# Hybrid decoder step on one core: order of bias, gather and first products in the experts' sums

## What is computed

```python
def expert_block(args):
    xb, e = args
    gu = xb @ w_gate_up[e] + b_gate_up[e]
    gt, up = gu[..., :D_EXPERT], gu[..., D_EXPERT:]
    gt = jnp.minimum(gt, SWIGLU_LIMIT)
    up = jnp.clip(up, -SWIGLU_LIMIT, SWIGLU_LIMIT)
    act = (up + 1) * (gt * jax.nn.sigmoid(gt * SWIGLU_ALPHA))
    return act @ w_down[e] + b_down[e]
...
out = jnp.zeros((N + 1, D), jnp.float32).at[slot_tok].add(ys.astype(jnp.float32) * slot_gate[:, None])[:N]
```

## Time and profile before

| | |
|---|---|
| median of 3 runs | 1282.88 us (1281.44 to 1283.17) |
| span of the profiled execution | 1278.8 us; an own time of that execution is not given |
| PE busy | 1208.2 us (94%) |
| DVE, ACT, POOL busy | 341.3, 208.4, 87.1 us |
| all transfers | 458.76 MB, mean 359 GB/s |
| chain that ended last | PE 62%, DMA 29%, DVE 5%, ACT 2% |

### The profile page before, as it was taken

The page is one execution under the profiler, slowest core; times in us unless marked ns, Lnnn a source line. Parts: engine busy times, 40 slices in busy tenths (PEclk is TensorE's granted clock), DMA queues, the critical chain, the costliest instruction groups (busy, mean ns, idle before and its releaser), DMA issues.

```text
span 1278.8 us, 18587 instructions
## 1 busy us (share of the span) xinstructions
PE 1208.2 (94%) x7592; PEld 594.0 (46%) x7592; DVE 341.3 (27%) x655; ACT 208.4 (16%) x421; POOL 87.1 (7%) x64
## 2 busy tenths in 40 slices
PE   6999999989999999999998989899898989898997
PEld 5877789875543433434333333324242433333332
DVE  1068497466411111111111111011111111111102
ACT  3133253320310111011011001000110101010002
POOL 0162003711000000000000000000000000000001
PEclk9999999999999999999999999999999999999999
DMA  9878460148699999999999999999999999999994
GB/s 316 197 249 283 144 222 12 37 177 322 279 379 427 428 428 425 429 427 428 426 428 427 427 426 429 428 426 427 429 428 426 427 428 427 428 427 428 428 426 190
DMA packets 52656, 458.76 MB, mean 359 GB/s; under 512 B 7092, under 2 KB 10844, under 8 KB 28004
## 3 DMA queue, kind: packets, MB, share of 16 engines
q1 hardware_dynamic: 49972, 452.22, 86.1%
q0 software_dynamic: 1824, 5.12, 1.7%
q10 hardware_dynamic: 784, 0.28, 0.1%
HBM read 453.74 MB, written 3.82 MB: 358 GB/s over the span
## 4 chain that ended last, share of the span: by engine, by line
PE 62%; DMA 29%; DVE 5%; ACT 2%; POOL 1%; issue 1%; SPq 0%; DVEq 0%; ACTq 0%; POOLq 0%
DMA ring<-in_w_gate_up 29%; PE ps L1901 24%; PE ps L1414 9%; PE ps L1922 7%; PE ps L1834 6%; PE ps L1881 3%; PE ps L1739 2%; PE ps L1843 2%; PE ps L1910 1%; DVE work L916 1%; PE ps L1390 1%; PE ps L1726 1%; DVE ring L916 1%; DVE work L954 1%; PE ps L1667 1%
## 5 line engine op out<-in xcount | busy, mean ns | idle before, releaser
L1901 PE MATMUL ps<-ring,work 128*64 128x512 f32 x1456 | 328.2, 598 | 32.0 <-DMA ring<-in_w_gate_up 30.0
L1901 PEld LDWEIGHTS ps<-ring,work 128*64 128x64 f32 x1456 | 101.3, 137 | 237.4 <-issue 192.6
L1304 DVE TENSOR_SCALAR work<-ps 128x512 f32<-128x512 f32 x32 | 22.1, 692 | 528.6 <-PE ps L1901 528.6
L1414 PE MATMUL ps<-work,ring 128*128 128x264 f32 x672 | 156.4, 392 | 2.2 <-ACT work L551 2.2
L1901 PE MATMUL ps<-work 128*64 128x512 f32 x592 | 132.7, 594 | 10.5 <-DMA work<-in_w_gate_up 10.5
L1414 PEld LDWEIGHTS ps<-work,ring 128*128 128x128 f32 x672 | 127.7, 192 | 28.2 <-issue 6.7
L1922 PE MATMUL ps<-ring,work 128*64 128x512 f32 x608 | 137.5, 597 | 0.2
L1922 PE MATMUL ps<-work 128*64 128x512 f32 x416 | 93.3, 594 | 0.2 <-DMA work<-in_w_down 0.2
L1322 DVE SCALAR_TENSOR_TENSOR work<-work 128x512 f32<-128x512 f32 x32 | 24.0, 751 | 241.0 <-ACT work L787 241.0
L1901 PEld LDWEIGHTS ps<-work 128*64 128x64 f32 x592 | 42.3, 137 | 94.0 <-issue 87.6
L1922 PEld LDWEIGHTS ps<-ring,work 128*64 128x64 f32 x608 | 41.3, 137 | 93.2 <-issue 89.6
(11 more groups left out here) (276 smaller groups left out, 900.1 us busy)
## 6 DMA issues: line engine op xcount, KB each, us to landing
ring<-in_w_gate_up SPq DMA_DIRECT2D x91, 2048.0 KB, 36.5
ring<-in_w_down SPq DMA_DIRECT2D x38, 2048.0 KB, 40.1
work<-in_w_gate_up SPq DMA_DIRECT2D x37, 2048.0 KB, 36.8
work<-in_w_down SPq DMA_DIRECT2D x26, 2048.0 KB, 39.5
ring<-in_w_in SPq DMA_DIRECT2D x5, 3072.0 KB, 16.6
ring<-in_w_out SPq DMA_DIRECT2D x1, 4096.0 KB, 13.0
ring<-in_w_in SPq DMA_DIRECT2D x2, 1536.0 KB, 8.7
ring<-in_cache_k SPq DMA_DIRECT2D x16, 192.0 KB, 7.5
```

Of the source, the lines that this page charges most:

```text
L1304: v.tensor_scalar(gt, PS[BG][:, :], LIMIT, None, ALU.min).then_inc(S_("gt"), 1)
L1414: last_ = mm(psum(job, T), w, hT[:, k, :], start=k == 0, stop=k == KD - 1)
L1901: last = mm(PS[bnk][g * 64:g * 64 + 64, :], lhs, UNIT[n % 9][:, w0 + base + g * 512:w0 + base + (g + 1) * 512], start=False, stop=k == KD - 1)
```

## The change

Three things are moved. (1) The gate and up sums now open with their first product (start=True at k = 0), and `bias` adds to them after k = 1, in both experts; `first_bias` and the bias calls between the stages are gone. (2) The second half of a pair's gather is no longer done in the pair before, but in the pair's own first `gate_up`, right behind the bias; ACT's copy of it moves to the head of the pair. (3) Ahead of the first pair, the sample rows' b_down term goes to bank BY in place of BU, and DVE makes the gates before it adds that term.

```diff
--- before.py
+++ after.py
@@ -748,18 +748,17 @@
                 nc.scalar.activation(gsT[g * 64:g * 64 + NE], PS[BX][0:NE, 0:NB], ACT.Copy).then_inc(S_("gate_s_out"), 1)
             route_exp(2)
 
-            def gathered(P, half, count, b=BX):
+            def gathered(P, half, count):
 
                 act.wait_ge(S_("xg_full"), count)
                 nc.scalar.activation(XG[P % 2][:, half, :, :, OWN:SLOT],
-                                     PS[b][:, :].rearrange("p (c e s) -> p c e s", c=4, e=2)[:, :, :, OWN:SLOT], ACT.Copy)\
+                                     PS[BX][:, :].rearrange("p (c e s) -> p c e s", c=4, e=2)[:, :, :, OWN:SLOT], ACT.Copy)\
                   .then_inc(S_("xgT_out"), 1)
 
             for h_ in range(2):
                 for e_ in range(2):
                     A_(nc.scalar.activation(XG[0][:, h_, :, e_, 0:OWN], h2T[:, 4 * h_:4 * h_ + 4, S:T], ACT.Copy))
-            for h_ in range(2):
-                gathered(0, h_, h_ + 1, (BX, BY)[h_])
+            gathered(0, 0, 1)
             for h_ in range(2):
                 A_(nc.scalar.activation(XG[1][:, h_, :, :, 0:OWN], XG[0][:, h_, :, :, 0:OWN], ACT.Copy))
 
@@ -790,13 +789,13 @@
                 with act.Fori(0, NE // 4) as four:
                     for q in range(2):
                         pr = act.snap(p * (NE // 2) + four * 2 + q)
+                        gathered(q, 1, pr * 2 + 2)
                         sigmoid(pr * 2)
                         gathered(q + 1, 0, pr * 2 + 3)
                         act_transposed(pr * 2)
                         act.wait_ge(S_("selgT_full"), pr + 1)
                         nc.scalar.activation(selgT_e[0], PS[BY][:, 0:256], ACT.Copy)
                         nc.scalar.activation(selgT_e[1], PS[BY][:, 256:512], ACT.Copy).then_inc(S_("selgT_out"), 1)
-                        gathered(q + 1, 1, pr * 2 + 4)
                         sigmoid(pr * 2 + 1)
                         expert_rows(pr * 2, pr * 12 + 19)
                         act_transposed(pr * 2 + 1)
@@ -1286,12 +1285,12 @@
             V(v.tensor_scalar(thr, marks, mcount, None, ALU.is_lt))
             V(v.tensor_reduce(mcount, thr, AX.X, ALU.add))
             V.ready(v.tensor_copy(npass[:, :], mcount), "npass", 1)
+            gates(1)
+            gates(2)
             dve.wait_ge(S_("samp_bias"), 1)
             dve.wait_ge(S_("samp_x"), 2)
-            V(tt(accs[0:NB], PS[BU][0:NB, :], accs[0:NB], ALU.add))
-            V.ready(tt(accs[64:64 + NB], PS[BU][64:64 + NB, :], accs[64:64 + NB], ALU.add), "samp_out", 1)
-            gates(1)
-            gates(2)
+            V(tt(accs[0:NB], PS[BY][0:NB, :], accs[0:NB], ALU.add))
+            V.ready(tt(accs[64:64 + NB], PS[BY][64:64 + NB, :], accs[64:64 + NB], ALU.add), "samp_out", 1)
 
             for b in range(1, PASSES):
                 V(v.tensor_scalar(posx[:, :, b * NE:(b + 1) * NE], posx[:, :, 0:NE], float(-FREE * b), None, ALU.add))
@@ -1827,11 +1826,11 @@
             pe.wait_ge(S_("sel_r"), 3)
             mm(rk[:, 1, :], C["before"], selr[:, 1, :], start=False, stop=False)
             done(mm(rk[:, 2, :], C["ones"], selr[:, 1, :], start=False, stop=True), "rk")
-            def gather(half, b=BX):
+            def gather(half):
 
                 for c in range(4):
                     for m in range(2):
-                        last = mm(PS[b][:, c * 128:(c + 1) * 128], h2[:, m, half * 512 + (c // 2) * 256 + c % 2:half * 512 + (c // 2 + 1) * 256:2],
+                        last = mm(PS[BX][:, c * 128:(c + 1) * 128], h2[:, m, half * 512 + (c // 2) * 256 + c % 2:half * 512 + (c // 2 + 1) * 256:2],
                                   sel[:, m].rearrange("p e s -> p (e s)"), start=m == 0, stop=m == 1)
                 last.then_inc(S_("xg_full"), 1)
 
@@ -1840,31 +1839,20 @@
                 pe.wait_ge(S_("pick"), count)
                 for i, g in ((0, 0), (1, 1), (0, 1), (1, 0)):
                     q = slice(i * NE, (i + 1) * NE)
-                    mm(PS[(BG, BU)[i]][g * 64:g * 64 + 64, :], pick[q, :], ebias[q, g * 512:(g + 1) * 512], start=True, stop=False)
-
-            def first_bias(i):
-
-                bank_free((BG, BU)[i])
-                q = slice(i * NE, (i + 1) * NE)
-                for g in range(2):
-                    mm(PS[(BG, BU)[i]][g * 64:g * 64 + 64, :], pick[q, :], ebias[q, g * 512:(g + 1) * 512], start=True, stop=False)
+                    mm(PS[(BG, BU)[i]][g * 64:g * 64 + 64, :], pick[q, :], ebias[q, g * 512:(g + 1) * 512], start=False, stop=False)
 
             pe.wait_ge(S_("gate_s_out"), 2)
             pe.wait_ge(S_("ld_bdown"), 32)
-            bank_free(BU)
+            bank_free(BY)
             for g in range(2):
                 q = slice(g * 64, g * 64 + NE)
-                last = mm(PS[BU][g * 64:g * 64 + NB, :], gsT[q], yS[q, :], start=True, stop=True)
+                last = mm(PS[BY][g * 64:g * 64 + NB, :], gsT[q], yS[q, :], start=True, stop=True)
             last.then_inc(S_("samp_bias"), 1)
-            pe.wait_ge(S_("pick"), 1)
-            pe.wait_ge(S_("ld_ebias"), 32)
-            first_bias(0)
             pe.wait_ge(S_("sel"), 1)
             gather(0)
-            bank_free(BY)
-            gather(1, BY)
-            pe.wait_ge(S_("samp_out"), 1)
-            first_bias(1)
+            pe.wait_ge(S_("ld_ebias"), 32)
+            bank_free(BG)
+            bank_free(BU)
             pe.wait_ge(S_("xgT_out"), 1)
             pe.wait_ge(S_("gate"), 3)
             for m in range(2):
@@ -1887,9 +1875,12 @@
             def gate_up(i, e_, pr, landed):
 
                 for k in range(KD):
-                    if e_ and k == 4:
-                        pe.wait_ge(S_("actT_out"), pr * 2 + 2)
-                        gather(1)
+                    if k == 2:
+                        bias(pr * 2 + 1 + e_, pick_e[e_])
+                        if e_ == 0:
+                            pe.wait_ge(S_("actT_out"), pr * 2 + 1)
+                            pe.wait_ge(S_("selgT_out"), pr + 1)
+                            gather(1)
                     if e_ == 0 and k % 4 == 0:
                         pe.wait_ge(S_("xgT_out"), pr * 2 + 1 + k // 4)
                     n, w0 = 12 * i + 4 * e_ + k // 2, (k % 2) * 2048
@@ -1899,7 +1890,7 @@
                     for bnk, base in ((BG, 0), (BU, 1024)):
                         for g in range(2):
                             last = mm(PS[bnk][g * 64:g * 64 + 64, :], lhs,
-                                      UNIT[n % 9][:, w0 + base + g * 512:w0 + base + (g + 1) * 512], start=False, stop=k == KD - 1)
+                                      UNIT[n % 9][:, w0 + base + g * 512:w0 + base + (g + 1) * 512], start=k == 0, stop=k == KD - 1)
                     if k % 2:
                         last.then_inc(S_("unit_used"), 1)
 
@@ -1930,8 +1921,6 @@
                 pe.wait_ge(S_("sel_next"), pr * 4 + 4)
                 pe.wait_ge(S_("actT_out"), pr * 2 + 1)
                 gather(0)
-                pe.wait_ge(S_("up"), pr * 2 + 1)
-                bias(pr * 2 + 2, pick_e[1])
                 pe.wait_ge(S_("xgT_out"), pr * 2 + 3)
                 act_T(pr * 2 + 1)
                 pe.wait_ge(S_("selg"), pr * 4 + 4)
@@ -1940,11 +1929,9 @@
                 last.then_inc(S_("selgT_full"), 1)
                 gate_up(i, 1, pr, landed)
                 pe.wait_ge(S_("selgT_out"), pr + 2)
-                down(i, 0, landed, range(0, 4))
-                pe.wait_ge(S_("up"), pr * 2 + 2)
-                bias(pr * 2 + 3, pick_e[0])
-                down(i, 0, landed, range(4, KD))
-                pe.wait_ge(S_("xgT_out"), pr * 2 + 4)
+                pe.wait_ge(S_("samp_out"), pr * 2 + 1)
+                pe.wait_ge(S_("actT_out"), pr * 2 + 2)
+                down(i, 0, landed)
                 act_T(pr * 2 + 2)
                 combine(pr + 2, pr * 2 + 2, selgT_e[0])
                 pe.wait_ge(S_("actT_out"), pr * 2 + 3)
```

## The result

| | before | after |
|---|---|---|
| median, same session | 1281.74 us (1278.36 to 1289.19, 20 runs) | 1286.89 us (1280.72 to 1292.52, 20 runs) |
| ratio | | 1.0041, 95% interval 1.0028 to 1.0054 |
| own time of the profiled execution | not given | 1285.53 us |
| its span, mean granted clock | 1278.8 us, 0.996 | 1283.7 us, 0.994 |

The change makes the kernel slower by 0.41%, 5.1 us. The forecast was no difference. Lines of after are one lower than those of before up to L1833; further down gate and up products are L1892 (before L1901), down L1913 (before L1922), `act_T` L1901, the gates' transposes L1859, the sample term L1849.

A forecast was written before the change was run, and what follows sets the result against it. Transfers bound the kernel: what counts is when their stream runs without a hole and PE's lag behind its last unit. +0.87 (unit 13's request) - 0.8 (end) = +0.1 us, giving 1282.9 us; range 1281.0 to 1284.9.

The forecast's parts named there:

- It starts 1.9 us earlier: Ahead of the first pair: two biases and one gather half go, two waits come; first expert at 351.45, 1.9 us earlier.
- no earlier start: Rival, ahead of the first pair: the wait for BY or `ebias` eats the lead; +2.0 us at worst, 1284.9; chance 0.08.
- Unit 0 was priced at 3.65: First pair's first weight unit: its products were taken at 3.65 us.
- Bias and gather half in front of unit 1: First pair's second weight unit stands behind bias (1.02 us) and gather half (2.08): 3.1 - 1.9 = 1.2 us later.
- shape switches: Rival, ahead of unit 1's products: three uncovered matmul shape changes cost 0.8 us each; +3.3 us, 1286.2; chance 0.08.
- The turn to the second expert: Within a pair: removing 1.02 us of bias between gather and transposes uncovers ACT's copy, so only 0.33 us is gained.
- Unit 13's request sets the stream, one for one: First pair's second expert: unit 13 asked for 0.87 us later, so the transfer stream runs 0.87 us later from there.
- Cheap restart: Rival, at unit 13: a just-drained queue lands requests faster than 8.5 us; -0.8 us, 1282.1, or -1.5; chance 0.15.
- Pairs and end: Pairs 54.7 us apart while PE is ahead; at the end only 0.8 us gained before PE waits at unit 189.
- The base: Starting time of the whole kernel: median 1282.88 us of three runs, 4.1 above the profiled span, an offset that stays.
- the prediction's own signs of a wrong step: First product after 352.5, no rate dips before 390, or last landing over 1.5 us from 1263.4 would prove a step wrong.

The follow-up runs named there:

- e5: Kernel before with three filler matmuls (0.88 us each) ahead of the sample term, starting the expert stage 2.6 us later; 1284.85 us, ratio 1.0026.
- e7: Kernel before with only the sample term in BY, gates first on DVE, second gather half behind up bias and `samp_out`; 1286.08 us, ratio 1.0041.
- e10: e7 plus one filler matmul ahead of the sample term; 1283.67 us, ratio 1.0018.
- e11: Changed kernel with the load of the number of passes moved up to right behind the first gather half; 1286.81 us, ratio 1.0038.
- e2: Kernel before with only the bias part of the change: bias behind k = 1, first products open the sums; 1283.56 us, ratio 1.0016.
- e6: e1 with the second expert's bias behind k = 5 instead of k = 1; 1282.76 us, ratio 1.0016.
- e8: Kernel before with bias behind k = 1, both gather halves ahead of first pair, passes load between them, later pairs' gathers moved, gates first; 1280.50 us, ratio 0.9998.
- e1: Changed kernel with three filler matmuls: ahead of the sample term, behind the first gather half, behind the gates' transposes; 1282.98 us, ratio 1.0018.
- after_again: Changed kernel once more, unchanged, in a later session; 1287.55 us, ratio 1.0052.
- e4: Changed kernel with the sample term back in bank BU and first products waiting for `samp_out`; 1284.78 us, ratio 1.0029.

## Why the prediction was wrong

Step by step, in the prediction's order.

1. **"It starts 1.9 us earlier" failed.** It said 351.45, which is 5.67 us behind unit 8's request; it was 8.80. Of the 3.13 us, 1.46 is the gather half at half clock, 1.20 the load and entry, which the sum left out (no row of before shows them: PE still had the queued gather and bias to work off while they went by), and 0.47 small differences around sample term and ACT's copy. Each piece of the sum was a row, but a row at full clock with its neighbours queued. I added the waits as lengths of time and did not ask what an idle PE does to the matmuls behind it. The rival "no earlier start" had the place right and capped the loss of lead at 1.9; the real one was larger.
2. **Unit 0 was priced at 3.65** and took 5.35, for the same reason: +1.70. With step 1 this makes unit 9's request 4.85 later than forecast (14.32 against 9.47).
3. **Bias and gather half in front of unit 1: right** (3.10 forecast; 359.05 to 362.14 is 3.09). The shape switches showed nothing; that rival, which had the time about right at 1286.2, had the wrong mechanism.
4. **The turn to the second expert: right.** Forecast 0.33 gained, measured 0.3. In all, unit 13 was asked for 5.90 later than before instead of 0.87: 3.13 + 1.70, and 0.2 at unit 1, whose use moved by 3.26 against unit 0's where the lengths of bias and gather half had given 3.10.
5. **"Unit 13's request sets the stream, one for one": nearly.** e5 shows it for a plain delay. In after the stream moved 6.57 for 5.90. From the request of unit 13 to the landing of unit 14 the kernels with the old order inside the pair (before, e5, e7, e10) took 13.5 to 14.3 us and the others 14.1 to 14.9, e11 15.8 and e2 16.9. An earlier request of unit 14 did not shorten it (e6). What decides it stays open: e8 and e11 gained 2.8 and 1.5 us at the request and kept 0.65 and 0.2 to 0.7 of it. "Cheap restart" was wrong: unit 9 landed in 7.6 us and unit 13 in 8.1, both faster than in before, and it did not help, as the requests were later.
6. **Pairs and end: right.** From the second on, pairs stand 54.5 us apart (forecast 54.7), PE waits for unit 189 in the last pair (1.15 us), and the end gives back 0.8.
7. **The base was 1.1 us too high.** The forecast of 1282.9 stood on the median of three runs, 1282.88; over 20 runs it is 1281.74. And the 4.1 us between that median and the profiled span were not an offset that stays: wherever both are on record, an execution's time is 1.7 to 1.9 us above its own span.

Two of the prediction's own signs of a wrong step came: the first product stood at 353.76 (after 352.5), and the last landing at 1269.1 (more than 1.5 us from 1263.4).

The sum that the runs support: +3.1 + 1.7 + 0.9 + 0.2 (requests), +0.7 (stream, no more than such executions differ by), -0.8 (end) = +5.8 behind unit 8's request, and 5.1 in the medians. Without the clock and most of the entry (e1) it is 1.8 by the medians (interval 0.6 to 4.1). So even a full clock leaves the change slower, not equal: the pair's inner order asks for unit 13 later, as the prediction said, while the earlier start was to pay for it and, by e1, pays 0.4 of the 1.9.

## What to carry to other kernels

When an edit takes matmuls out ahead of a wait, price what stands behind the wait at half clock too, and look for what the removed work was hiding on the same queue: here a register load and a loop entry of 1.2 us. An idle of little more than a microsecond, at a place where buffers are about to come free, cost more than the work that was saved; a dummy matmul in the gap is a quick test of it. And where a deep stream of transfers follows the uses of its buffers, ask of every edit when the first late buffer comes free, since the stream keeps that delay to the end.

## What the runs showed of the hardware

- The granted clock fell to 0.50 behind an idle of 1.36 us (after, after_again, e7, e11) and stayed at 1.00 where one matmul cut it to 0.42 (e1, e10). e2 had a gap of 1.21 us ahead of its first product and kept the full clock; e4, with 0.90 and 2.27, did not. From 348 to 350 and from 350 to 352 us PE was busy for 2.00 and 0.63 us in e2, for 1.10 and 0.32 us in e4. So the gap alone does not decide; where the border lies was not tried.
- Low stretches come elsewhere too, in before near 266 us and at 1156 us, there behind a wait of 2.42 us for weights. In the middle of the stream the slower unit left the transfer rate at 422 GB/s.
- In e11 one moved load changed which operations ran at half clock: gather and sample term instead of gather and unit 0.
- A 2 MB request (units 9 and 13) landed 7.6 and 8.1 us after its issue in after where before has 9.0 and 8.5; over all fourteen profiles the two took 7.6 to 10.2.
- In e5 a plain delay of 2.65 us at the request of unit 13 was still 2.69 us at the last landing, 178 units later.
